# Modulation sums moved wholly to VectorE, latent roots and rotated queries moved ahead in the heads, first MLP tiles of block 2 by column halves

## The reference, cut to what matters

```python
# block 1, layer i
h = rmsnorm(x, mix_norm[i]); z = h @ w_in[i]          # u, gelu gate, c_q, ckv + k_rope, fq, fk, fv, f, gates
y_a = rglru(u, ...) @ w_br_a[i]                       # linear recurrence over the tokens (wa, wx gates)
q  = rmsnorm(c_q, q_norm) @ wuq                       # latents of 384; 8 heads of 64 + 32 rotated
kv = rmsnorm(c_kv, kv_norm) @ wukv                    # latents of 256
y_b = attention(q, k, v) @ w_br_b[i]
y_c = forget_attention(fq, fk, fv, f) @ w_br_c[i]
x = x + (g0 * y_a + g1 * y_b + g2 * y_c) @ w_o[i]
hf = rmsnorm(x, ffn_norm[i]) @ w_gate_up[i]           # 2 x 2816
x = x + (silu(hf[:, :2816]) * hf[:, 2816:]) @ w_down[i]
x = x + sigmoid(rmsnorm(x, ple_norm[i]) @ w_ple_gate[i]) * (p[i] @ w_ple[i])
# block 2: for the latents (c) and the context (c_ctx)
mod = silu(c) @ ada_w[l] + ada_b[l]                   # 1024 x 6144 per layer: 6 vectors of 1024
x = x + gate * pool_mix(modulate(norm(x), shift, scale))      # layer 0
x = x + gate * attention(modulate(norm(x), shift, scale))     # layer 1
x = x + gate * (square(relu(modulate(norm(x), shift, scale) @ w1)) @ w2)   # 1024 -> 4096 -> 1024
```

## Time and profile before

| what | value |
|---|---|
| median of 3 executions | 1834.68 us (1832.49 to 1835.5) |
| profiled execution, its own time | 1833.74 us |
| profiled execution, span | 1831.9 us |
| mean granted TensorE clock | 0.983 |
| VectorE, ScalarE, GpSimd busy | 891.2, 893.1, 1172.0 us |
| moved by DMA | 299.02 MB, mean 163 GB/s |

### The profile page before, as it was taken

The page is one execution under the profiler, slowest core; times in us unless marked ns, Lnnn a source line. Parts: engine busy times, 40 slices in busy tenths (PEclk is TensorE's granted clock), DMA queues, the critical chain, the costliest instruction groups (busy, mean ns, idle before and its releaser), DMA issues.

```text
span 1831.9 us, 32203 instructions
## 1 busy us (share of the span) xinstructions
PE 1738.3 (95%) x12690; PEld 1601.1 (87%) x12690; DVE 891.2 (49%) x2019; ACT 893.1 (49%) x1468; POOL 1172.0 (64%) x768
## 2 busy tenths in 40 slices
PE   6899999999999899999999969999999979889997
PEld 6788899999999788999999968888888778689997
DVE  6577445313365674353233666854444565642223
ACT  6545546444666455465445864232323353564443
POOL 6887678788878776677788623444444443058884
PEclk9999999999999899999999989999999999999999
DMA  6543465665555433666655503354453422035552
GB/s 238 192 144 127 133 236 190 226 212 184 176 188 185 154 128 129 235 200 214 219 185 175 199 26 127 140 194 163 171 183 139 172 93 81 24 116 186 182 184 81
DMA packets 83414, 299.02 MB, mean 163 GB/s; under 512 B 9152, under 2 KB 11456, under 8 KB 83008
## 3 DMA queue, kind: packets, MB, share of 16 engines
q1 hardware_dynamic: 81648, 294.02, 47.3%
q10 hardware_dynamic: 1616, 2.95, 0.5%
HBM read 295.89 MB, written 1.05 MB: 162 GB/s over the span
## 4 chain that ended last, share of the span: by engine, by line
PE 84%; DVE 7%; ACT 3%; issue 2%; POOL 2%; DVEq 1%; DMA 1%; ACTq 0%; SPq 0%
PE bank L980 25%; PE bank L984 24%; PE bank L983 24%; POOL wlo L929 2%; PE bank L994 1%; PE bank L1146 1%; PE bank L1160 1%; PE bank L1252 1%; PE bank L1176 1%; ACT whi L1399 1%; PE bank L1223 1%; DVE acts L2103 1%; PE bank L1226 1%; PE bank L1227 1%; PE bank L1149 1%
## 5 line engine op out<-in xcount | busy, mean ns | idle before, releaser
L929 POOL TENSOR_TENSOR wlo<-raw,whi 128x256 fp32r<-128x256 f32 (+1 forms) x756 | 1166.3, 1567 | 638.9 <-ACT whi L1399 638.3
L980 PE MATMUL bank<-split_acts,whi 128*128 128x256 f32 (+1 forms) x3492 | 1058.6, 303 | 26.7 <-DVE split_acts L1859 16.0
L983 PE MATMUL bank<-split_acts,whi 128*128 128x256 f32 (+1 forms) x3492 | 1046.1, 300 | 0.0
L984 PE MATMUL bank<-split_acts,wlo 128*128 128x256 f32 (+1 forms) x3492 | 1046.0, 300 | 0.0
L1399 ACT ACTIVATE whi<-raw 128x1024 fp32r<-128x1024 f32 x459 | 483.6, 1056 | 550.4 <-DMA raw<-in_stream 302.8
L980 PEld LDWEIGHTS bank<-split_acts,whi 128*128 128x128 f32 x3492 | 669.4, 192 | 68.3 <-issue 24.0
L983 PEld LDWEIGHTS bank<-split_acts,whi 128*128 128x128 f32 x3492 | 670.3, 192 | 20.6
L984 PEld LDWEIGHTS bank<-split_acts,wlo 128*128 128x128 f32 x3492 | 669.8, 192 | 21.0
L1859 DVE TENSOR_TENSOR split_acts<-bank,split_acts 128x256 fp32r<-128x256 f32 (+1 forms) x214 | 98.7, 461 | 50.2 <-ACT split_acts L1543 20.9
L2525 DVE SCALAR_TENSOR_TENSOR acts<-bank,acts 128x256 f32<-128x256 f32 x104 | 47.4, 481 | 149.5 <-PE bank L984 149.0
L1907 DVE SCALAR_TENSOR_TENSOR acts<-raw,acts 128x512 f32<-128x512 f32 x112 | 111.9, 1019 | 8.1 <-issue 2.5
(11 more groups left out here) (277 smaller groups left out, 1610.5 us busy)
## 6 DMA issues: line engine op xcount, KB each, us to landing
raw<-in_stream SPq DMA_DIRECT2D x555, 512.0 KB, 3.6
acts<-in_x SPq DMA_DIRECT2D x1, 1024.0 KB, 6.1
acts<-in_ctx ACTq DMA_DIRECT2D x1, 1024.0 KB, 7.3
acts<-in_const ACTq DMA_DIRECT2D x1, 1024.0 KB, 5.2
out<-acts SPq DMA_DIRECT2D x8, 128.0 KB, 2.1
acts<-in_const SPq DMA_DIRECT2D x1, 711.0 KB, 8.2
acts<-in_p ACTq DMA_DIRECT2D x2, 256.0 KB, 3.9
acts<-in_const ACTq DMA_DIRECT2D x1, 320.0 KB, 3.0
```

Of the source, the lines that this page charges most:

```text
L929: last = nc.gpsimd.tensor_tensor(wlo[slot][:, cols], raw[source][:, cols], whi[slot][:, cols].bitcast(F32), ALU.subtract)
L980: first = nc.tensor.matmul(out_ap, w_hi, hi_act(k), start=(k == 0), stop=False)
L983: nc.tensor.matmul(out_ap, w_hi, lo_act(k), start=False, stop=False)
L984: last = nc.tensor.matmul(out_ap, w_lo, hi_act(k), start=False, stop=(k == k_tiles - 1))
```

## The change

Three edits.

1. All 12 modulation vectors are summed on VectorE. There are now 96 mod chunks: 24 in the feed-forward of each layer of block 1 (before hg(0,1) to hg(0,9), dn(0,1) to dn(0,6), hg(1,0) to hg(1,8)), and 48 in block 2's first MLP. The ada and turn tiles are gone. Four chunks make one half vector (512 outputs). In block 1 its two partial sums (one per sample) lie in PSUM, in a bank each; in block 2 one is in SBUF, one in PSUM. A half ends in one reduction per sample that also transposes (L1923, 128 x 512 into 128 x 16, columns of `folded`). Each stage (layer 0, layer 1, block 2) has a single sum tile, two tiles behind its last mod chunk, with 4 small matmuls and a drain. A mod chunk is fetched four tiles later in the stream than the place at which it is summed (`fetch_tiles`).
2. In the heads, ss q and ss kv stand between wa and wx, ScalarE's roots ahead of the last wx's splits, and the reciprocals right behind rcol. The queries to be rotated come behind vm: qr0, qr1, kn0, kn1, rotq0, rotq1, kn2, kn3, qn0 to qn3. The scores wait for their own qn tile to be out of its bank; `mla_ready` is gone.
3. The first three w1 tiles of block 2 (BY_SIDE) are done by column halves: the context's 256 columns of all three, k by k, interleaved with the eight norm sums of the latents, and then the latents' columns (`first_by_side`).

Beside these, the context's squares have 2 buffers in place of 4, and `opening_gains` comes after hu(1,9) in place of after the first half's dn tiles.

```diff
@@ HEAD_TILES @@
-    + [("wa", j) for j in range(4)] + [("wx", j) for j in range(4)]
-    + [("col", "mix"), ("fv", 0), ("fv", 1), ("ss", "q"), ("ss", "kv")]
+    + [("wa", j) for j in range(4)] + [("ss", "q"), ("ss", "kv")] + [("wx", j) for j in range(4)]
+    + [("col", "mix"), ("fv", 0), ("fv", 1)]
     + [("rotk", 0), ("col", "kv"), ("vm", 0), ("vm", 1)]
-    + [("kn", j) for j in range(4)] + [("qn", j) for j in range(4)] + [("qr", 0), ("qr", 1)]
-    + [("rotq", 0), ("rotq", 1)])
+    + [("qr", 0), ("qr", 1), ("kn", 0), ("kn", 1), ("rotq", 0), ("rotq", 1), ("kn", 2), ("kn", 3)]
+    + [("qn", j) for j in range(4)])
...
+FFN_PLACES = {**{("hg", 0, j): 1 for j in range(1, 10)}, **{("dn", 0, n): 1 for n in range(1, 7)},
+              **{("hg", 1, j): 1 for j in range(9)}}
...
 MLP_PLACES = [((w, 0, q, j), 1) for q in range(QUARTERS)
-              for w, js in (("w1", range(2, 7) if q == 0 else range(1, 6)),
-                            ("w2", range(8 if q < 2 else 7 if q == 2 else 5))) for j in js]
+              for w, js in (("w1", range(5, 7) if q == 0 else range(1, 7)),
+                            ("w2", range(8 if q < QUARTERS - 1 else 4))) for j in js]
@@ TensorE @@
+            def sum_quadrants(b, stage):
+
+                pe.wait_ge(mod_summed, stage + 1)
+                n = len(SUM_SLOTS[stage])
+                parts = folded[:, 0:16 * n].rearrange("p (m q) -> p m q", q=4)
+                for q in range(4):
+                    nc.tensor.matmul(b[32 * q:32 * q + 32, 0:4 * n], C("fold"), parts[:, :, q], start=True, stop=True)
+                return pe.drain()
...
-                        if i == 0:
-                            pe.wait_ge(mla_ready, lay + 1)
+                        if qb == 0:
+                            out_of_bank(("qn", m))
...
+                for k in range(KT):
+                    for i in {0: range(4), 2: (4, 5), 4: (6, 7)}.get(k, ()):
+                        summed = norm_sum(i)
+                    if k == 4:
+                        summed.then_inc(gemm_done, 1)
+                    pe.wait_ge(m_split, 16 + k + 1)
+                    for j, t in enumerate(BY_SIDE):
+                        if k == 0:
+                            banks.append(open2(t))
+                        if k in (0, CHUNK_ATOMS // 2):
+                            pe.wait_ge(lo_ready, (at + k) // CHUNK_ATOMS + j + 1)
+                        step(0, j, k)
+                for k in range(KT):
+                    pe.wait_ge(m_split, 24 + k + 1)
+                    for j in range(3):
+                        first, last = step(1, j, k)
...
@@ ScalarE, heads @@
+                root("q")
+                root("kv")
                 keep_ahead(("wx", 3))
...
                 keep_ahead(("fv", 0))
-                root("q")
-                root("kv")
@@ VectorE @@
                     for s in sides:
-                        w, total = raw[c % RING][:, k % 2 * 512:(k % 2 + 1) * 512], mod_sums[half % 2][s]
+                        w = raw[c % RING][:, k % 2 * 512:(k % 2 + 1) * 512]
                         factor = silu_c[:, 2 * k + s:2 * k + s + 1]
                         if k == 0:
-                            last = v.tensor_scalar(total, w, factor, None, ALU.mult)
+                            last = v.tensor_scalar(parts[s], w, factor, None, ALU.mult)
                         else:
-                            last = v.scalar_tensor_tensor(out=total, in0=w, scalar=factor, in1=total, op0=ALU.mult,
-                                                          op1=ALU.add)
+                            last = v.scalar_tensor_tensor(out=parts[s], in0=w, scalar=factor, in1=parts[s],
+                                                          op0=ALU.mult, op1=ALU.add)
                 last.then_inc(mod_used, 1)
                 if pair == SUM_CHUNKS - 1:
-                    v.drain().then_inc(mod_summed, 1)
+                    v.drain()
+                    for s in sides:
+                        i = SUM_SLOTS[stage].index((half, s))
+                        last = v.tensor_reduce(folded[:, 16 * i:16 * i + 16],
+                                               parts[s].rearrange("p (b j) -> p b j", j=32), axis=AXX, op=ALU.add,
+                                               apply_transpose=True)
+                    if half == STAGE_SUMS[stage][-1]:
+                        last.then_inc(mod_summed, 1)
...
                 b = arrived(("col", "mix"))
                 left(v.tensor_copy(rcol[:, 0:2], b[:, 0:2]), ("col", "mix"))
+                latent_rstd("q", yt, rstd_q)
+                latent_rstd("kv", gt[:, 0:256], rstd_kv)
                 v.drain()
                 lru_core(0)
...
-                norm_rstd("q", rstd_q, 384)
-                norm_rstd("kv", rstd_kv, 256)
```

More of the change, by code:

```diff
@@ L135, in modulation_before @@
     for t in tiles:
-        if t[0] in ("ada", "turn", "mod", "sum"):
+        if t[0] in ("mod", "sum"):
             run.append(t)
@@ L412, in shape_constants @@
     put(c, CONST, "sub", np.stack([(i // 32) % 2 == 0, (i // 32) % 2 == 1], 1))
-    put(c, CONST, "strips", np.stack([i == 32 * s + sample for s in range(4) for sample in range(2)], 1))
+    put(c, CONST, "fold", np.tile(np.eye(32), (4, 1)))
     d = np.zeros((P, NCONST2), np.float32)
@@ L481, in layer_atoms @@
     for t in TILES:
-        if t in SHARED or t[0] in ("ada", "turn"):
+        if t in SHARED or t[0] == "sum":
             continue
@@ L952, in _ @@
                 atom = 0
-                ada = 0
             def weights(n):
@@ L1040, in gemm @@
                     b = open_bank(t)
-                    if kind == "ada":
-                        modulation(b)
-                        pe.drain().then_inc(gemm_done, 1)
-                        return
-                    if kind == "turn":
-                        out_of_bank(("ada", PLACES * j + PLACES - 1))
-                        turn_rows(b, rows).then_inc(gemm_done, 1)
+                    if kind == "sum":
+                        sum_quadrants(b, lay).then_inc(gemm_done, 1)
                         return
@@ L1248, in gemm2 @@
                 elif kind == "sum":
[L1249 to L1253 removed]
+                    last = sum_quadrants(b, SECOND)
                 elif kind == "py":
@@ L2379, in _ @@
                 for t in MID_TILES:
-                    if t[0] not in ("ada", "turn"):
-                        of_tile(t)
+                    of_tile(t)
                 merged_lo(7)
```

299 lines of the change are left out of this document (143 added, 156 removed).

## The result

The changed kernel runs in 1802.53 us (median of 4, 1800.49 to 1804.1) against 1835.09 us (median of 4) for the kernel before: a ratio of 0.983, 95% interval 0.981 to 0.985. So it is 32 us faster where 54 were forecast.

A forecast was written before the change was run, and what follows sets the result against it. TensorE, busy 95% of the span, was taken as the bound. Heads -25.6, modulation -22.2 and -14.55, new sum tiles +2.7, VectorE +14 and block 2's opening -8 sum to -53.7 us: 1781 us, range 1767 to 1803.

The forecast's parts named there:

- the attention behind the heads: Block 1's attention from first scores to feed-forward, without its ada tiles: no change, 0 us.
- the term "+14": Block 1's feed-forward: VectorE some 5 us late at layer 0's sum tile and 9 at layer 1's, +14 us.
- Step 1: Block 1's heads: earlier roots and rotated queries bring the scores forward 11.2 and 14.4 us, -25.6 in sum.
- rival (c): Block 1's heads give half, ScalarE's tables or GpSimd holding vm: -12 instead of -25.6, 1794 us; chance 0.12.
- Step 2: Modulation off TensorE: ada and turn tiles -22.2 us, block 2's old sums -14.55, three new sum tiles +2.7.
- Step 3: Block 1's feed-forward: VectorE's added work takes 5.60 of a pair's 5.76 us, plus 1.48 of reductions per half; +14 us.
- rival (b): PSUM sums do not keep VectorE out of GpSimd's way: 48 chunks at 5.54 us, not 2.97; about 1904; chance 0.04.
- Step 4: Opening of block 2's first MLP: context half done before the latents' splits; -8 us, at most 10.7.
- rival (a): VectorE sets the feed-forward's pace: +16 us, or +31 with both causes; 1797 as middle, 1790 to 1812; chance 0.18.

The follow-up runs named there:

- e3: Changed kernel with block 1's heads back in their old order (latent sums and roots behind fv, rotated queries last): 1800.53 us.
- e1: Changed kernel with GpSimd waiting once per layer until the first two softmax units of the MLA attention are normalised: 1786.44 us.
- e2: Changed kernel with each layer's first two normalisations as a product of two SBUF tensors instead of a per-partition scaling: 1798.8 us, one run.
- e9: Changed kernel with GpSimd taking the chunks behind the head whole instead of in four pieces: 1808.5 us, one run.
- e7: Changed kernel with GpSimd's pause, block 1's sum tile one pair later, and modulation chunks fetched 2 tiles behind their places instead of 4: 1779.3 us.
- e10: Changed kernel with only the modulation chunks fetched 2 tiles behind their places instead of 4: 1799.07 us.
- e5: Changed kernel with the old heads and the old opening of block 2's first MLP, so the modulation's move alone: 1810.52 us.
- e4: Changed kernel with block 1's sum tile before hg(1,10) instead of hg(1,9): 1789.22 us.

## Why the prediction was wrong, step by step

Two steps failed: the attention behind the heads, which the sum has at nothing without a reason, and the term "+14" for VectorE in the feed-forward.

**Step 1, heads: the mechanism and the size were right, what follows was not asked.** Scores at 100.1 for 99.6; layer 1 gained 13.7 for 14.4. The sum ended there. The first scaling behind the scores now falls into GpSimd's unbroken run and takes 9 us: 13.5 us lost with the slow clock behind it (13.3 against e3's kernel). That GpSimd's run is what holds it is shown by e1, e2, e3 and e9; why this one is starved and others in such a run are not stays open. The forecast read GpSimd's run only as a pace (3.12 us a chunk). The question it left out was which VectorE operations on SBUF the move would put beside it. The forecast's phrase on rival (c), that GpSimd might hold the heads, had the right engine and the wrong way: vm did not wait for it.

The Trainium skill, page "SBUF — State Buffer", section "Who interferes with whom", says that VectorE and GpSimd share a port pair under an exclusive lock, which an operation of VectorE needs in a two-port mode or with two inputs from SBUF, and that the second to issue is blocked until the first is done. The scalings that get in mid-run, 0.55 us for 0.28 alone, would fit that. The starved ones do not: the wait is longer than one operation, 13 GpSimd pieces went ahead of one waiting scaling (102.76 to 111.99, 0.7 us apart), and the wait ended where GpSimd had none ready. For an operation with two SBUF inputs (e2) it was the same.

**Step 2, work off TensorE: right, and 1.6 us too small.** An ada tile was worth 1.39 us for 1.30, since the second product behind it also came late (341.96 to 342.18, for 0.12), and a turn 0.42 for 0.36: 23.8 for 22.2. The old sums were 15.0 for 14.55. Block 2's opening and sums together gave 22.6 for 21.65.

**Step 3, VectorE in the feed-forward: a size.** The term "+14", with 1.8 for the two sum tiles 15.8, measured 24.9. The prices of the operations held: four accumulations are 2.90 us beside GpSimd (2.97 forecast), the transposing reductions 1.31 a pair (1.48 forecast), and the rival (b) fell; in block 2, where one sum stayed in SBUF, the same operation costs half again as much. Groups of VectorE, with the mean ns of one:

```profile
L1916 DVE SCALAR_TENSOR_TENSOR bank<-raw,acts,bank 128x512 f32<-128x512 f32 x252 | 182.0, 752 | 36.3 <-DMA raw<-in_stream 24.8 <-issue 0.6
...
L1916 DVE SCALAR_TENSOR_TENSOR acts<-raw,acts 128x512 f32<-128x512 f32 x28 | 31.9, 1141 | 2.4 <-issue 0.2
...
L1914 DVE TENSOR_SCALAR bank<-raw,acts 128x512 f32<-128x512 f32 x36 | 25.9, 750 | 2.0 <-issue 0.3
L1923 DVE TRANSPOSE_TENSOR_REDUCE acts<-bank 128x16 f32<-128x512 f32 x36 | 24.2, 698 | 1.8
```

What failed was the time of a pair, forecast at 5.60 and measured at 5.80. The wait of 0.45 us for ScalarE's split is in the forecast's 2.14 already and has not changed. What grew is the step before it. Before, VectorE took hg's product (L2202) one tile ahead of hu's, so ScalarE's activation of hg was done before L2205, and L2207 followed 0.34 behind. Now VectorE takes both in one go, the activation can start only behind L2212, and L2217 follows L2215 after 0.54 (436.23, 436.77 above). VectorE and ScalarE before, and ScalarE in e7:

```profile
341.20 0.41 DVE L2207 SCALAR_TENSOR_TENSOR acts<-acts,bank 128x256 f32<-128x256 f32 x1
```

```profile
338.45 0.38 ACT L1539 ACTIVATE acts<-bank 128x256 f32<-128x256 f32 x1
```

```profile
436.36 0.39 ACT L1550 ACTIVATE acts<-bank 128x256 f32<-128x256 f32 x1 [1.31 <-DVE bank L2212]
```

The chain is 2.37 for 2.14, and two hand-overs of 0.09 and 0.10 come on top; the accumulations (2.90 for 2.97) and the first add (0.34 for 0.49) give 0.22 back: 2.90 + 0.09 + 0.34 + 2.37 + 0.10 = 5.80. With 0.16 of slack per pair there is little lateness, with -0.04 there is no recovery. The gaps of the two feed-forwards sum to 18.3 us (8.4 and 9.9) where 14 were forecast. Some 5 more are neither gap nor sum tile. Most of them are the clock, which was granted at 0.72 and 0.75 in the 13 us around layer 0's idle time at the sum tile, between 1.2 and 2.4 GHz, and at 1.00 before and after; 7 us at 0.75 are 1.75 us less work, and layer 1's window behind its idle time, at 0.78, costs nearly as much. The forecast priced gaps without the slow clock behind them. The price of fetching four tiles late was forecast as nothing; VectorE waited 24.8 us for it, which cost TensorE at most 3.5 us (e10). The window behind the idle time:

```profile
453.00:460.00 7.00, 6.90 (x51) 6.72 (x51) 2.49 (x8) 3.16 (x5) 3.91 (x2) 0.75 0.63 222
```

**Step 4, block 2's opening: right**, 8 forecast, 8.4 measured between the traces of the two kernels, 7.8 between those of e5 and e3.

**The range.** The result lies at its slow end, 1803, and 21 us from the forecast. The slow side was built from the feed-forward (rival (a), up to 1812) and the heads (rival (c), 1794) one at a time. An overrun of the feed-forward by 9 and a loss of half the heads' gain, neither by the mechanism of its rival, came together with a clock dip.

## What to carry to other kernels

When an edit moves a chain earlier, list what each engine does beside its new place, not only what it waits for: an operation may be ready and still not run. Where GpSimd works through a backlog without a break, give it one wait, on the very result that the critical engine needs, at the start of a unit that nobody needs soon: pauses of 0.60 and 3.20 us ended gaps of 5.37 and 4.10 us, worth 4.9 us in each layer when what came back later is taken off. When an engine is loaded to within a few per cent of the one that it feeds, count its period from start to start in the new order of its work, since a partner's step that used to be done ahead may now be waited for, and try the reader of a long sum further back: two tiles more gave 10.1 us here (e4).
